# Doubling inverse of the delta rule's 128-token blocks: the transposed inverse taken by transpositions of T, and one unit of filling on either side of each level's T product

## The reference, cut to what matters

```python
decay = jnp.exp(jnp.where(causal, gc[..., :, None] - gc[..., None, :], -jnp.inf))
kb = k * beta[..., None]
low = jnp.where(strict, jnp.einsum('nbhid,nbhjd->nbhij', kb, k) * decay, 0.0)
a_mat = low + jnp.eye(C, dtype=f32)
rhs = jnp.concatenate([v * beta[..., None], kb * jnp.exp(gc)[..., None]], -1)
sol = lax.linalg.triangular_solve(a_mat, rhs, left_side=True, lower=True, unit_diagonal=True)
u, w = sol[..., :dv], sol[..., dv:]
...
def step(S, xs):
    q_i, k_i, u_i, w_i, a_i, gl = xs
    v_new = u_i - jnp.einsum('bhcd,bhde->bhce', w_i, S)
    o = jnp.einsum('bhcd,bhde->bhce', q_i, S) + jnp.einsum('bhij,bhje->bhie', a_i, v_new)
    S = S * jnp.exp(gl)[..., None, None] + jnp.einsum('bhcd,bhce->bhde', k_i, v_new)
    return S, o
```

## Time and profile before

| what | value |
|---|---|
| median of 3 runs | 1606.64 us (1602.61 to 1607.3) |
| the profiled execution's own time | 1606.99 us |
| its span | 1605.3 us |
| TensorE busy | 1489.8 us, 93% of the span |
| VectorE busy | 920.9 us, 57% |
| ScalarE busy | 627.1 us, 39% |
| mean granted TensorE clock | 0.977 of full |
| the eight heads of the delta rule | from 68 to about 485 us, one head every 52 us |

### The profile page before, as it was taken

How to read it: one execution, slowest core, us unless ns; L and a number is a source line. 1 busy time by engine, 2 the same in 40 slices (tenths; PEclk the granted TensorE clock), 3 DMA queues, 4 the chain that set the end, 5 groups by cost and what they waited for, 6 DMA issues and landing times.

```text
span 1605.3 us, 20981 instructions
## 1 busy us (share of the span) xinstructions
PE 1489.8 (93%) x7458; PEld 1212.1 (76%) x7458; DVE 920.9 (57%) x1322; ACT 627.1 (39%) x989; POOL 134.6 (8%) x121
## 2 busy tenths in 40 slices
PE   6899999999887899999999899999896999999997
PEld 5688877887675888888788686566576888887886
DVE  5555665466446566666422626989875666665225
ACT  3743455345512344444311234454522444444120
POOL 4101110011002000000000201111010000000002
PEclk8999999999998899999999999999998999999999
DMA  5211121121021133333332121112111233333231
GB/s 162 65 42 47 46 59 26 46 59 47 27 79 40 39 105 92 91 105 118 106 104 92 53 79 45 48 39 65 63 56 53 79 105 91 94 102 128 100 100 66
DMA packets 157726, 118.85 MB, mean 74 GB/s; under 512 B 5898, under 2 KB 145644, under 8 KB 157676
## 3 DMA queue, kind: packets, MB, share of 16 engines
q1 hardware_dynamic: 157676, 118.17, 24.5%
HBM read 116.04 MB, written 2.11 MB: 74 GB/s over the span
## 4 chain that ended last, share of the span: by engine, by line
PE 72%; DVE 12%; issue 6%; ACT 5%; POOL 2%; DMA 1%; SPq 1%; ACTq 0%; DVEq 0%; POOLq 0%
PE bank L1457 12%; PE bank L1458 12%; PE bank L1459 12%; PE bank L1445 7%; PE bank L1447 7%; PE bank L1446 7%; PE bank L1520 5%; PE bank L1513 3%; PE bank L1787 2%; DVE w_lo L329 1%; ACT w_hi L324 1%; PE bank L1475 1%; SPq L395 1%; DVE x_tok L1176 1%; DVE bn L1180 1%
## 5 line engine op out<-in xcount | busy, mean ns | idle before, releaser
L1457 PE MATMUL bank<-x_hi,w_hi 128*128 128x512 f32 (+1 forms) x1160 | 463.1, 399 | 29.3 <-DVE x_lo L930 25.8
L1459 PE MATMUL bank<-x_hi,w_lo 128*128 128x512 f32 (+1 forms) x1160 | 442.4, 381 | 0.0
L1458 PE MATMUL bank<-x_lo,w_hi 128*128 128x512 f32 (+1 forms) x1160 | 441.7, 381 | 0.0
L329 DVE TENSOR_TENSOR w_lo<-raw,w_hi 128x1024 fp32r<-128x1024 f32 x196 | 246.7, 1262 | 319.9 <-ACT w_hi L324 307.1
L1457 PEld LDWEIGHTS bank<-x_hi,w_hi 128*128 128x128 f32 x1160 | 223.2, 192 | 69.6 <-DVE w_lo L329 24.2
L324 ACT ACTIVATE w_hi<-raw 128x1024 fp32r<-128x1024 f32 x188 | 197.0, 1050 | 192.4 <-PE bank L1447 155.6
L1459 PEld LDWEIGHTS bank<-x_hi,w_lo 128*128 128x128 f32 x1160 | 222.3, 192 | 41.7
L1458 PEld LDWEIGHTS bank<-x_lo,w_hi 128*128 128x128 f32 x1160 | 223.1, 192 | 37.2 <-issue 3.4
L1445 PE MATMUL bank<-w_hi,u_hi 128*128 128x512 f32 x416 | 167.0, 402 | 16.3 <-DVE w_lo L329 6.2
L1447 PE MATMUL bank<-w_hi,u_lo 128*128 128x512 f32 x416 | 164.6, 396 | 0.0
L1446 PE MATMUL bank<-w_lo,u_hi 128*128 128x512 f32 x416 | 164.4, 395 | 0.0
(11 more groups left out here) (270 smaller groups left out, 2018.7 us busy)
## 6 DMA issues: line engine op xcount, KB each, us to landing
raw<-in_ffn_w_up SPq DMA_DIRECT2D x88, 512.0 KB, 3.8
raw<-in_ffn_w_down SPq DMA_DIRECT2D x44, 512.0 KB, 3.3
raw<-in_gdn_w_in SPq DMA_DIRECT2D x32, 512.0 KB, 4.1
raw<-in_diff_w_in SPq DMA_DIRECT2D x24, 512.0 KB, 3.7
raw<-in_gdn_w_out SPq DMA_DIRECT2D x8, 512.0 KB, 3.5
raw<-in_diff_w_out SPq DMA_DIRECT2D x8, 512.0 KB, 3.5
x_tok<-in_x SPq DMA_DIRECT2D x4, 512.0 KB, 5.9
ROW<-decay_rows SPq DMA_DIRECT2D x8, 256.0 KB, 4.6
```

The lines of the kernel that those rows point to most:

```text
L329: nc.vector.tensor_tensor(w_lo[:, s, :], raw[:, (base + r) % RAW, :], w_hi[:, s, :].bitcast(F32), ALU.subtract).then_inc(lo_ready, 1)
L1457: nc.tensor.matmul(out, hi, x_hi[:, k, cols], start=(k == 0), stop=False)
L1458: nc.tensor.matmul(out, hi, x_lo[:, k, cols], start=False, stop=False)
L1459: ins = nc.tensor.matmul(out, lo, x_hi[:, k, cols], start=False, stop=last)
```

## The change

The second T product and its add disappear from levels 2 to 32. Instead, at the next level, right behind P, TensorE transposes the updated `TM` into X(e, 2) (`four(2, at(TM), None, turn=True)`), and VectorE copies the half of it that is new into `TT` before this level's T product. Level 64 keeps its transposed product. One unit of filling moves from ahead of the T product to behind it (level 2: from 3 ahead to 2 ahead and 1 behind; the others from 2 ahead to 1 and 1). The two places in the numbering of semaphores follow.

```diff
-LV = [f"{k}{s}" for s in LEVELS for k in ("P", "T", "TT") if (k, s) != ("T", LEVELS[-1])]
+LV = [key for i, s in enumerate(LEVELS)
+      for key in [f"P{s}"] + ([f"TT{LEVELS[i - 1]}"] if i else []) + [f"T{s}" if i < len(LEVELS) - 1 else f"TT{s}"]]
...
                     s = LEVELS[i]
+                    if i > 0:
+                        pe(f"TT{LEVELS[i - 1]}")
+                        new = halves(TT[e][:, :, :].rearrange("p n t -> p (n t)"), LEVELS[i - 1], 1)
+                        nc.vector.tensor_copy(new, halves(X(e, 2)[:, :], LEVELS[i - 1], 1)).then_inc(d_dve, 1)
                     if i < len(LEVELS) - 1:
                         pe(f"T{s}")
                         old = halves(TM[e][:, :, :].rearrange("p n t -> p (n t)"), s, 0)
                         nc.vector.tensor_tensor(old, halves(X(e, 1)[:, :], s, 0), old, ALU.add).then_inc(d_dve, 1)
-                    pe(f"TT{s}")
-                    old = halves(TT[e][:, :, :].rearrange("p n t -> p (n t)"), s, 1)
-                    nc.vector.tensor_tensor(old, halves(X(e, 2)[:, :], s, 1), old, ALU.add).then_inc(d_dve, 1)
+                    else:
+                        pe(f"TT{s}")
+                        old = halves(TT[e][:, :, :].rearrange("p n t -> p (n t)"), s, 1)
+                        nc.vector.tensor_tensor(old, halves(X(e, 2)[:, :], s, 1), old, ALU.add).then_inc(d_dve, 1)
...
                     four(0, at(LT), at(TM))
-                    n_fill = 3 if i == 0 else 2
+                    if i > 0:
+                        four(2, at(TM), None, turn=True)
+                    n_fill = 2 if i == 0 else 1
                     fill(p, p + n_fill)
                     p += n_fill
                     dve(f"P{s}")
...
                     if s != LEVELS[-1]:
                         part(1, TT, PB, s, 0)
-                    part(2, PB, TT, s, 1)
+                    else:
+                        part(2, PB, TT, s, 1)
+                    fill(p, p + 1)
+                    p += 1
                     if more and s == LEVELS[3]:
                         square_sum(h + 1, 1 - e, 0)
```

## The result

The changed kernel takes 1628.21 us (median of 4 runs, 1625.56 to 1629.58) against 1605.82 before (median of 4 runs, 1602.61 to 1607.3): 1.0143 times as long, 95% interval 1.0127 to 1.0159. It is slower by 22, where 27 was forecast. The profiled execution took 1625.56, its span 1623.8; the granted clock is 0.972 on the mean.

The account below looks back on a forecast made before the run. TensorE was taken to bound the eight heads, with VectorE's mask, copy and tap now delaying its T products. Levels 16.7, last head 1.5 and clock 9.1 sum to 27.3, so 1607.0 becomes 1634 us, range 1622 to 1644.

Parts of the forecast that it names:

- What bounds the kernel: In the eight delta-rule heads, TensorE holds 72% of the chain; its time saved or waited reaches the end almost one for one.
- The levels: Heads 0 to 6, levels 2 to 64: -0.15, +1.83, +0.51, -0.15, -0.09, +0.43; 2.38 a head, 16.7 in seven.
- The last head: No tap, but lumpy filling: levels 8, 16 and 32 lose 0.54 each, about 1.5 us together.
- The clock: Level 4's idle of about 2.3 halves TensorE's clock in each of seven heads, 1.3 each, 9.1 us in all.
- The count of nine in ten: Of ten TensorE stalls of this size after 50 us in the timeline, all but the one at 443.22 had the fall.
- The rival that the clock holds: At level 4 the stalls come but TensorE stays at full clock: 1625 us; chance 0.18.
- The rule of the Trainium skill: Advises avoiding only idle gaps between bursts longer than level 4's stall; by it TensorE's clock would hold.
- the rival of two falls a head: Level 8's idle of 0.88 less 0.17 holds or renews the half clock, another 1.3 a head: 1643 us; chance 0.10.
- The total: Whole kernel: 27.3 us added to 1607.0, giving 1634 us.
- The faster rival: The copy never holds TensorE up, its saving decides: -1.6 a head, -12.8 for eight, 1594 us; chance 0.09.

Follow-up runs that it names:

- the second profile of the changed kernel: The changed kernel measured once more, unaltered: 1631.66 us, 1.0164 times the kernel before.
- e7: The changed kernel with nine extra matmuls of 512 columns, result unused, in level 4's wait in heads 0 to 6: 1623.05 us, 1.0112 of before.
- e1: The changed kernel with VectorE's copy right behind the mask, at level 4 also the add to T ahead of the taps: 1603.45 us, 0.9994 of before.
- e3: The kernel before with only the filling split, one unit moved behind the T products, both products kept: 1624.68 us, 1.0132 of before.
- e6: e5 with the last head's filling units cut in halves: 1593.99 us, 0.9928 of before.
- e5: e1 with filling relaid: three units ahead, one behind at level 2; two ahead at 16; one ahead at 64; others one and one: 1595.47 us, 0.9943 of before.
- e2: The changed kernel with transpositions and copies kept but the filling back ahead of the T product: 1629.17 us, 1.0163 of before.

## Why the prediction was right

**What bounds the kernel.** Right. TensorE's distance from P to P grew, and the end moved with it: from the first product of head 0 to that of head 7 it is 390.4 against 367.7, +22.7 in the profile (25.8 forecast, with the clock), and +24.3 in the second profile of the changed kernel.

**The levels.** Right to 0.1 at each: heads at full clock, as all seven in e7, show -0.16, +1.82, +0.49, -0.24, -0.15 and +0.40. Their sum is 2.2 a head, where 2.38 was worked out; a product behind mask and copy started 2.20 after its P (231.37 and 233.57 in e1), not 2.23, and level 16 gave a little more than forecast. The copy was put at 0.42 and took 0.415 on the mean of 40.

**The last head.** +1.5 forecast. In the second profile of the changed kernel it is +1.2 up to the first product with RV; in the first it is +4.0, because there the clock fell at a stall of 2.91 on weights ahead of level 2 (half from 463.27 to 470.09), the one which had left the clock alone before (at 443.22).

**The clock.** Right in kind, somewhat too large in count. I took a fall in each of seven heads at 1.3. It came in five and in six, at 1.4 and 1.5 a fall. That the mean lies so near the forecast is in part luck: it took the half clock to begin about 1 after the work resumes, and it began anywhere from just ahead of that (by 0.1) to 1.8 behind it, so that single falls cost 0.8 to 2.3. The count of nine in ten also rested on two stalls of 12, which say little of one of 2.2. The rival that the clock holds is refuted by these profiles, and e7 shows what it would have given: 1623, against 1625 as worked out. The rule of the Trainium skill that was set beside it ("TensorE: Matmul & The Clock Gate", why this matters for your kernels) would not have warned of gaps of this length. A half clock of 6.8, which is what the rival of two falls a head would show, came once in each profile (head 1, then head 2), and levels 4 and 8 took 12.9 there instead of 10.7. It is not that rival's mechanism, though: it was one stretch that began with the work behind level 4, and in these two heads TensorE had no idle time at level 8 (0.00 instead of 0.64).

**The total.** In the profiled executions the span grew by 18.5: 22.7 in heads 0 to 6 (25.8 forecast; the levels came 1.5 below the forecast and the clock in them 2.3, and 0.7 came on top outside the levels), 4.0 in the last head, less 2.0 ahead of the heads (head 0 starts at 65.96, not 67.97) and less 6.2 behind them. The last two lie outside of the change; without them the profile would have grown by 26.7, against the 27.3 forecast. Behind the heads, the granted clock was half for 41 in the first profile of the changed kernel and for 54 before. All the profiles bear this out, since the program there is nearly the same in each: from the last head's first product with RV to the end it takes 1128.8 with 41 at half clock (changed), 1130.5 and 1132.0 with 48 (e1, e7), 1132.8 with 51 (e3, e6), and 1134.2 to 1135.0 with 54 to 58 (the other five, the second profile of the changed kernel and the kernel before among them). Why the clock falls there more often in one profile than in another is not shown, nor what the 2.0 ahead of the heads is.

**The faster rival.** It was stated with its condition, q complete or the queue out of the way, and 1594. e1, which meets the condition in another way, gives 1603 with its fillings where the change put them; only with e5's layout does the saving of the transpositions show, 1595. So the rival's sum was too large for this change: it left out that mask and copy take 2.23 even without a tap (2.20 measured in e1), more than the 2.01 of TensorE, and that the last head loses (+1.2) instead of gaining 1.6.

## What to carry to other kernels

When an operand is made later than before, look for what stands ahead of its maker in that engine's queue, and at what releases that; here a copy of 0.4 behind a tap released by the very work just ahead of the waiting product cost 2.2 a head at level 4 (6.1 against 3.9 in e1). An edit that loses by itself, as the split filling does, may still pay with another, so cost the pair, and lay the filling by the chain it has to cover: one unit behind the product where the add to T would otherwise hold TensorE (0.52 in e2), none where other work already stands there (the square sum at level 16). A stall of 2 us on TensorE should be priced with the fall of its clock, on the mean another 1.4 to 1.5 for each fall here, and keeping TensorE busy with useless work won that back.

## What the runs showed of the hardware that was not expected

- Idle time alone doesn't decide the fall of the clock. The idle 2.20 to 2.21 at level 4, at the same place of the program, came with half clock in 10 of 12 cases (heads 0 to 5 of both profiles of the changed kernel), and in other heads from one profile to the next; 1.99 in head 6 in 1 of 2; 1.51 in 3 of 6 (e2); about 1.2 (0.95 in head 0) in one of seven in e3 and in none of seven in e1, at the same level 2.
- The small 32-bit products lose as much by the half clock as the filling: in head 3, P took 1.91 instead of 1.09 and four transpositions 1.06 instead of 0.60, where a matmul of 512 columns (L1463) took 0.78 instead of 0.48.
- The product with 64 columns costs about as much as one with 128: 0.81 to 0.94 for four T products against 0.81 to 0.99 for the four of P, from start to next start at full clock. Four transpositions of 128 columns behind P cost 0.35 or 0.36.
